# Units of the S5 scan by chunk instead of by quad, and the imaginary sum of each unit on VectorE

## The reference, cut to what matters

```
bu_re = einsum('btgc,gpc->btgp', u, bbar_re);  bu_im likewise
h_t = abar * h_(t-1) + bu_t           (complex, diagonal; associative_scan over t)
y = einsum('btgp,gcp->btgc', h_re, c_re) - einsum('btgp,gcp->btgc', h_im, c_im)
y = gelu(y + d_skip * x);  z = y @ w_glu + b_glu;  out = z[:, :D] * sigmoid(z[:, D:])
```

## Time and profile before

| | |
|---|---|
| median of 3 runs | 1521.61 us (1520.65 to 1522.02) |
| profiled execution | 1522.97 us, its span 1521.1 us |
| TensorE | 1483.9 us busy, 98% of the span |
| VectorE | 1033.6 us, 68% |
| ScalarE | 320.8 us, 21% |
| GpSimd | 90.3 us, 6% |
| chain that ended last | 92% TensorE, 4% VectorE, 2% GpSimd |
| mean granted clock of TensorE | 0.995 of full speed |

### The profile page before, as it was taken

The page is one execution under the profiler, slowest core; times in us unless marked ns, Lnnn a source line. Parts: engine busy times, 40 slices in busy tenths (PEclk is TensorE's granted clock), DMA queues, the critical chain, the costliest instruction groups (busy, mean ns, idle before and its releaser), DMA issues.

```text
span 1521.1 us, 56639 instructions
## 1 busy us (share of the span) xinstructions
PE 1483.9 (98%) x25360; PEld 1098.6 (72%) x25360; DVE 1033.6 (68%) x3653; ACT 320.8 (21%) x598; POOL 90.3 (6%) x71
## 2 busy tenths in 40 slices
PE   9998999999999799999999999999999999999997
PEld 8887889999999687666666666666666666668664
DVE  7787546896875514776766766766667767766665
ACT  2733225677442012001001001001001001001001
POOL 0006202000002700000000000000000000000000
PEclk9999999999999899999999999999999999999999
DMA  8230004444531493979989989989989989999991
GB/s 328 91 131 3 4 4 168 167 167 167 174 132 45 181 390 131 368 273 419 415 327 417 415 332 412 414 340 405 416 345 399 416 351 386 416 362 375 415 368 56
DMA packets 74690, 422.98 MB, mean 278 GB/s; under 512 B 6848, under 2 KB 6976, under 8 KB 39504
## 3 DMA queue, kind: packets, MB, share of 16 engines
q1 hardware_dynamic: 74096, 418.27, 69.5%
q0 software_dynamic: 352, 1.10, 0.2%
HBM read 418.29 MB, written 1.05 MB: 276 GB/s over the span
## 4 chain that ended last, share of the span: by engine, by line
PE 92%; DVE 4%; POOL 2%; issue 1%; ACT 1%; DVEq 0%; POOLq 0%
PE PS L1338 38%; PE PS L1346 19%; PE PS L1147 11%; PE PS L1263 3%; PE PS L776 2%; PE PS L753 2%; PE PS L1370 1%; PE PS L720 1%; PE PS L1132 1%; PE PS L924 1%; PE PS L797 1%; DVE ZI L1608 1%; PE PS L941 1%; PE PS L1253 1%; POOL SPS L2075 1%
## 5 line engine op out<-in xcount | busy, mean ns | idle before, releaser
L1338 PE MATMUL PS<-EXA,XGT 128*32 128x256 f32 x10752 | 611.5, 379 | 0.0
L1965 DVE STREAM_TRANSPOSE MHT<-MHF 32x32 f32<-32x32 f32 x2688 | 544.9, 203 | 40.1
L1338 PEld LDWEIGHTS PS<-EXA,XGT 128*32 128x32 f32 x10752 | 352.6, 110 | 223.1 <-issue 0.4
L1346 PE MATMUL PS<-EXB,MHT 128*32 128x256 f32 x5376 | 321.3, 379 | 1.6 <-DVE MHT L1965 1.6
L1346 PEld LDWEIGHTS PS<-EXB,MHT 128*32 128x32 f32 x5376 | 176.5, 110 | 114.6 <-DVE MHT L1965 2.1
L1960 DVE TENSOR_TENSOR MHF<-MSG,PS 128x128 f32<-128x128 f32 x168 | 48.4, 288 | 239.4 <-ACT MSG L670 238.7
L670 ACT ACTIVATE MSG<-PS 128x128 f32<-128x128 f32 x168 | 46.6, 277 | 764.8 <-PE PS L1338 758.8
L1147 PE MATMUL PS<-FH,WHI 128*128 128x256 f32 x352 | 100.4, 285 | 0.0
L1147 PE MATMUL PS<-FL,WHI 128*128 128x256 f32 x352 | 99.6, 283 | 0.0
L1147 PE MATMUL PS<-FH,WLO 128*128 128x256 f32 x352 | 99.5, 283 | 0.0
L1147 PEld LDWEIGHTS PS<-FH,WHI 128*128 128x128 f32 x352 | 67.5, 192 | 0.2 <-issue 0.2
(11 more groups left out here) (417 smaller groups left out, 1767.8 us busy)
## 6 DMA issues: line engine op xcount, KB each, us to landing
EXA<-in_wmoe SPq DMA_DIRECT2D x112, 2048.0 KB, 18.0
EXB<-in_wmoe SPq DMA_DIRECT2D x224, 512.0 KB, 14.5
FRA<-in_wffn SPq DMA_DIRECT2D x22, 1024.0 KB, 6.0
RING<-in_wsq SPq DMA_DIRECT2D x16, 1024.0 KB, 5.0
FRB<-in_wffn SPq DMA_DIRECT2D x22, 512.0 KB, 3.8
GLUW<-in_wglu SPq DMA_DIRECT2D x8, 1024.0 KB, 12.7
LORA<-in_lora SPq DMA_DIRECT2D x1, 1536.0 KB, 19.3
CON<-in_con SPq DMA_DIRECT2D x1, 1156.0 KB, 21.6
```

The lines of the kernel that those rows point to most:

```text
L1338: mm = pe.matmul(PS[strip(a), GU_BANK[r], 0:T], XGT[:, k, strip(s)], EXA[(2 * quad + e // 2) % RA][:, e % 2, k * T:(k + 1) * T], start=k = ...
L1346: mm = pe.matmul(PS[strip(a), 2 + r // 2, r % 2 * 256:(r % 2 + 1) * 256], MHT[:, i % RB * SLOTS + 32 * s:i % RB * SLOTS + 32 * s + 32], EX ...
L1965: tr = dve.transpose(MHT[strip(q), first:first + 32], MHF[strip(a), strip(q)])
```

## The change

Units 0 to 3 now hold one chunk each (unit c has the four strips of chunk c); units 4 to 7 hold one strip of the four chunks of the second half, as before. The drive is cut up: `drive_chunk(c)` fills 128 columns of four banks (4 to 7 for chunk 1, otherwise 0 to 3), and `drive_quads` makes the second half two chunks at a time. `turn_by` reads units 0 to 3 across four banks, `read_out(0)` waits for one unit for each chunk, and GpSimd and VectorE wait before a slot of PQ only for the chunk that was read from it. VectorE gets the imaginary sum (`imaginary`), after the scans of the next unit; GpSimd makes the two products and the real sum. The tables are laid out in the new order. `first_level` uses banks 2 to 5 and no longer waits for `x_sb`. The core of the diff:

```
             def first_level(g):
-                bank = 2 + 2 * (g % 2)
+                bank = 2 + g
                 pe.wait_ge(S("lt"), g + 1)
-                if g >= 2:
-                    pe.wait_ge(S("x_sb"), g - 1)
...
-            def drive(part):
-                for cc in range(4):
-                    c = 4 * part + cc
-                    if part == 0 or cc == 0:
-                        pe.wait_ge(S("n_out"), 16 + (c + 1 if part == 0 else KC))
...
+            def drive_chunk(c):
+                pe.wait_ge(S("n_out"), 16 + (KC if c == 1 else c + 1))
+                if c >= 2:
+                    pe.wait_ge(S("s_lin"), c if c == 3 else 1)
+                for m in range(2):
+                    for i in range(STEP):
+                        for q in range(NQ):
+                            mm = pe.matmul(PS[:, 4 * (c == 1) + q, m * CHUNKS:(m + 1) * CHUNKS], BBT[STEP - 1 - i][strip(q), m, c, :],
+                                           by_step(HN[strip(q), c, :])[:, :, i], start=i == 0, stop=i == STEP - 1,
+                                           tile_position=(32 * q, 0), skip_group_check=True)
+                mm.then_inc(S("bu_ps"), 1)
+
+            def drive_quads(chunks):
+                pe.wait_ge(S("s_lin"), 2)
+                for c in chunks:
                     for m in range(2):
                         for i in range(STEP):
                             for q in range(NQ):
-                                first = m * T + cc * CHUNKS
-                                mm = pe.matmul(PS[:, 4 * part + q, first:first + CHUNKS], BBT[STEP - 1 - i][strip(q), m, c, :],
+                                first = m * T + (c - 4) * CHUNKS
+                                mm = pe.matmul(PS[:, 4 + q, first:first + CHUNKS], BBT[STEP - 1 - i][strip(q), m, c, :],
...
             def taps(part):
+                pe.wait_ge(S("s_lin"), NQ)
                 for c in range(4 * part, 4 * part + 4):
-                    pe.wait_ge(S("s_lin"), c // 2 + 1)
...
             def read_out(part):
-                pe.wait_ge(S("s_prod"), 16 * (part + 1))
                 for cc in range(4):
                     c = 4 * part + cc
+                    if part == 0:
+                        pe.wait_ge(S("s_prod"), 3 * (c + 1))
+                        pe.wait_ge(S("s_im"), c + 1)
+                    elif cc == 0:
+                        pe.wait_ge(S("s_prod"), 6 * NQ)
+                        pe.wait_ge(S("s_im"), 2 * NQ)
...
-            drive(0)
-            drive(1)
+            drive_chunk(0)
+            drive_chunk(1)
+            drive_chunk(2)
+            drive_quads((4, 5))
+            drive_chunk(3)
+            drive_quads((6, 7))
...
-                bu = PS[:, n, :].rearrange("p (a t) -> p a t", a=2)
                 for x, trig, done in ((SA, COS, "s_ab"), (SB_, SIN, "s_lin")):
-                    tt(x[:, v, :, :], bu, trig[:, n:n + 1, :].to_broadcast([P, 2, T]), ALU.mult).then_inc(S(done), 1)
+                    if n < NQ:
+                        first = 4 if n == 1 else 0
+                        bu = PS[:, first:first + NQ, 0:2 * CHUNKS].rearrange("p q (m t) -> p m q t", m=2)
+                        dest = x[:, v, :, :].rearrange("p m (q t) -> p m q t", q=NQ)
...
+            def imaginary(n):
+                dve.wait_ge(S("s_prod"), 3 * n + 2)
+                if n >= NQ:
+                    dve.wait_ge(S("yq_ps"), n - NQ + 1)
+                tt(PQ[:, n % NQ, 1, :], SPS[:, 0, :], SPC[:, 1, :], ALU.add).then_inc(S("s_im"), 1)
...
                 scan(n)
+                if n > 0:
+                    imaginary(n - 1)
                 if n < 2 * NQ - 1:
                     rotate(n + 1)
+            imaginary(2 * NQ - 1)
...
                 if n > 0:
-                    pool.wait_ge(S("s_prod"), 4 * n)
+                    pool.wait_ge(S("s_prod"), 3 * n)
+                    pool.wait_ge(S("s_im"), n)
                 for x, trig in ((SPC, COS), (SPS, SIN)):
                     tt(x[:, :, :], SGS[:, v, :, :], trig[:, n:n + 1, :].to_broadcast([P, 2, T]), ALU.mult).then_inc(S("s_prod"), 1)
                 if n >= NQ:
-                    pool.wait_ge(S("yq_ps"), 4)
-                pool.wait_ge(S("s_prod"), 4 * n + 2)
+                    pool.wait_ge(S("yq_ps"), n - NQ + 1)
+                pool.wait_ge(S("s_prod"), 3 * n + 2)
                 tt(PQ[:, q, 0, :], SPC[:, 0, :], SPS[:, 1, :], ALU.subtract).then_inc(S("s_prod"), 1)
-                tt(PQ[:, q, 1, :], SPS[:, 0, :], SPC[:, 1, :], ALU.add).then_inc(S("s_prod"), 1)
```

More of the change, by code:

```diff
@@ L1227, in drive @@
                             for q in range(NQ):
-                                first = m * T + cc * CHUNKS
-                                mm = pe.matmul(PS[:, 4 * part + q, first:first + CHUNKS], BBT[STEP - 1 - i][strip(q), m, c, :],
+                                first = m * T + (c - 4) * CHUNKS
+                                mm = pe.matmul(PS[:, 4 + q, first:first + CHUNKS], BBT[STEP - 1 - i][strip(q), m, c, :],
                                                by_step(HN[strip(q), c, :])[:, :, i], start=i == 0, stop=i == STEP - 1,
                                                tile_position=(32 * q, 0), skip_group_check=True)
-                                if cc == 3 and m == 1 and i == STEP - 1:
+                                if c == KC - 1 and m == 1 and i == STEP - 1:
                                     mm.then_inc(S("bu_ps"), 1)
             def taps(part):
+                pe.wait_ge(S("s_lin"), NQ)
                 for c in range(4 * part, 4 * part + 4):
-                    pe.wait_ge(S("s_lin"), c // 2 + 1)
                     for d in range(STEP):
@@ L1252, in read_out @@
                                 out = by_step(PS[strip(q), c // 2, c % 2 * T:(c % 2 + 1) * T])
+                                slot, first = (cc, q * CHUNKS) if part == 0 else (q, cc * CHUNKS)
                                 mm = pe.matmul(out[:, 1:CHUNKS, i], CW[:, i + 1, m, 4 * c + q, :],
-                                               PQ[:, q, m, cc * CHUNKS:(cc + 1) * CHUNKS - 1], start=False,
+                                               PQ[:, slot, m, first:first + CHUNKS - 1], start=False,
                                                stop=i == STEP - 1 and m == 1, skip_group_check=True)
@@ L1602, in _ @@
                 l, g = n0 // 4, n0 % 4
-                bank = 2 + 2 * (n0 % 2)
+                bank = 2 + g if l == 0 else 2 + 2 * (n0 % 2)
                 if l == 0:
@@ L1764, in table @@
                 sin, cos = SIN[:, n, :], COS[:, n, :]
-                tiles = [(slice(cc * CHUNKS, (cc + 1) * CHUNKS), 16 * (n // NQ) + 4 * cc + n % NQ) for cc in range(4)]
+                tiles = [(slice(cc * CHUNKS, (cc + 1) * CHUNKS), 4 * n + cc if n < NQ else 16 + 4 * cc + n - NQ) for cc in range(4)]
                 for own, j in tiles:
@@ L1809, in prepare @@
                     for part in range(2):
-                        own = MAG[:, NQ * part:NQ * part + NQ, :].rearrange("p q (c n) -> p q c n", c=4)
-                        mag = S5T[:, 20, 16 * part:16 * part + 16].rearrange("p (c q) -> p q c", q=NQ)
+                        own = MAG[:, NQ * part:NQ * part + NQ, :].rearrange("p u (b n) -> p u b n", b=4)
+                        mag = S5T[:, 20, 16 * part:16 * part + 16].rearrange("p (c q) -> p c q" if part == 0 else "p (c q) -> p q c", q=NQ)
                         link(dve.tensor_copy(own, mag.unsqueeze(3).to_broadcast([P, NQ, 4, CHUNKS])))
@@ L1846, in turn_by @@
                     dve.wait_ge(S("s_g"), 2 * n - 2)
-                bu = PS[:, n, :].rearrange("p (a t) -> p a t", a=2)
                 for x, trig, done in ((SA, COS, "s_ab"), (SB_, SIN, "s_lin")):
-                    tt(x[:, v, :, :], bu, trig[:, n:n + 1, :].to_broadcast([P, 2, T]), ALU.mult).then_inc(S(done), 1)
+                    if n < NQ:
+                        first = 4 if n == 1 else 0
+                        bu = PS[:, first:first + NQ, 0:2 * CHUNKS].rearrange("p q (m t) -> p m q t", m=2)
+                        dest = x[:, v, :, :].rearrange("p m (q t) -> p m q t", q=NQ)
+                        angle = trig[:, n, :].rearrange("p (q t) -> p q t", q=NQ).unsqueeze(1).to_broadcast([P, 2, NQ, CHUNKS])
+                    else:
+                        bu, dest = PS[:, n, :].rearrange("p (a t) -> p a t", a=2), x[:, v, :, :]
+                        angle = trig[:, n:n + 1, :].to_broadcast([P, 2, T])
+                    tt(dest, bu, angle, ALU.mult).then_inc(S(done), 1)
             def rotate(n):
@@ L1861, in scan @@
                 if n >= 2:
-                    dve.wait_ge(S("s_prod"), 4 * n - 6)
+                    dve.wait_ge(S("s_prod"), 3 * n - 4)
                 for m in range(2):
                     dve.tensor_tensor_scan(SGS[:, v, m, :], MAG[:, n, :], SA[:, v, m, :], 0.0, ALU.mult, ALU.add).then_inc(S("s_g"), 1)
+            def imaginary(n):
[3 more added lines that the diff above has]
```

(1 more changed line is left out.)

## The result

The changed kernel takes 1526.4 us (median of 20 runs, 1518.07 to 1534.27), the kernel before 1519.93 (20 runs, 1517.41 to 1522.68): a ratio of 1.0042 (95% interval 1.0023 to 1.0061), slower where 1512.7 us was forecast. The median hides the shape: ten runs lie between 1518 and 1523 us (median 1521.4), ten between 1530 and 1535 (median 1531.8), and none between. No run took 1526 us. The kernel before has one group. Four executions of the whole series, far off everything else (1564, 1896, 4364 and 5417 us), are disturbed and not used as evidence.

What follows compares the result with a forecast made beforehand. In the mixer both TensorE and the unit chain ended at 527.8, so both must come forward; last read-out from 527.84 to 518.9 gives 8.9 us, 1522.97 to 1514.1, less 1.36 for the median: 1512.7 us, range 1510.8 to 1516.4.

Steps and rivals of the forecast that it cites:

- The start of the units: Mixer: unit 0 needs one drive chunk instead of four, so GpSimd begins at 480.5 instead of 485.71, 5.2 us earlier.
- The time per unit: Mixer's GpSimd and VectorE cycle: 4.86 us per unit instead of 5.09, bounds 3.80 and 5.43; last unit done at 518.2.
- Rival 1: Mixer units: imaginary sum fully on VectorE's cycle, period 5.43, unit 7 ends at 522.2; gain 5.6, 1516.0 us; chance 0.22.
- TensorE's path: Drive, taps, first read-out and GLU half on TensorE without the 8 us hole, ending at 517.0 to 519.2.
- a wait of 0.7 for HN: Drive: after chunk 0 at 475.2 TensorE waits 0.7 us, then 448 records take 13.2 us, ending at 489.0.
- Rival 3: Drive and taps: late units 2 or 3 drop the clock to 0.50, +14 to +23 us, 1526 to 1535; chance 0.03.
- 3.96 us at clock 1.00, to 502.9, or 504.4 with the pause: First read-out: runs at once behind the taps at full clock, 3.96 us; the pause allowed for is 1.48 us.
- the 518.9 that went into the sum: Start of the last read-out, set somewhat later than units at 518.2 and TensorE at 517.0 to 519.2; before, 527.84.
- rival 2: First read-out: TensorE's instructions come slower than they run, two pauses of 1.48 us; gain 7.2, 1514.4 us; chance 0.16.
- The other edits: `first_level` without its VectorE wait: 0, bounds 0 and 0.3 us either way; table, magnitude and slot orders: 0.
- The old hole of 8 us: Kernel before: no matmul from 498.2 to 506.2; read-out behind it at clock 0.50 took 6.33 us, against 3.96 busy.

Runs made afterwards that it cites:

- experiment 2: Changed kernel with three more filler matmuls ahead of chunk 0 of the drive, so chunk 1 follows without a gap; 1522.87 us, ratio 1.0011.
- experiment 11: Changed kernel with filler matmuls, two GLU weight loads at the drive's end, six after the first read-out, imaginary sum back on GpSimd; 1517.52 us.
- experiment 12: Kernel before with one wait moved: chunk 1 of the drive waits for all of HN, a 0.43 us gap; 1532.88 us, ratio 1.0074.
- experiment 5: Changed kernel with filler matmuls and GLU weight loads in two lots, four at the drive's end, four after the first read-out; 1514.95 us, ratio 0.9956.
- 10: Changed kernel with weight loads in two lots of four, without the filler matmuls, so the gap is back; 1527.07 us, ratio 1.0025.
- experiment 4: Changed kernel with the imaginary sum back on GpSimd, gap ahead of chunk 1 still there; 1530.99 us, ratio 1.0057.
- experiment 3: Kernel before with the chunk solve's edit alone (`first_level` on four banks, no wait for VectorE); 1522.45 us, ratio 1.0004.
- experiment 6: Changed kernel with filler matmuls and all eight GLU weight loads only after the first read-out; 1520.15 us, ratio 0.999.
- experiment 7: Changed kernel with filler matmuls and all eight GLU weight loads when the dense FFN is done, beside norm and drive; 1526.6 us, ratio 1.0032.
- 9: Changed kernel with filler matmuls, two GLU weight loads at the drive's end and six after the first read-out; 1517.41 us, ratio 0.997.

## Why the prediction was wrong

**The start of the units: right.** In the changed kernel's trace VectorE's first product came 2.41 us after the drive's start (473.64 - 471.23); forecast 475.78 - 473.29 = 2.49. GpSimd began 478.60 - 471.23 = 7.4 us after it, forecast 7.2, and 6.9 in experiment 2, where the filler makes the drive later and not the units. The products that read four banks take 0.60 us each, as those with one bank: no extra cost.

**The time per unit: right.** Walked 4.86 us, measured 4.93, and 5.12 with the sum on GpSimd. The moved sum saves 0.19 us a unit. The last unit was done at 518.13 against 518.2. Rival 1 (a period of 5.43, with the sum fully on VectorE's cycle) is refuted, and in experiment 11 this part of the change has no worth at the end: the two kernels' medians are 0.1 us apart.

The page of the Trainium skill that doubted such a move (Perfetto Trace Analysis, Optimizing Scalar/DVE Operations) agrees in effect with the runs: 0.19 of 0.72 us is left, and nothing of it in the time.

**TensorE's path: here it failed, in two steps.** The step "a wait of 0.7 for HN" priced that wait at its own length. Rival 3 had the clock fall in the drive and stay low, with 1526 to 1535 us, which takes in the upper group. But it tied the fall to units that come late, and it was given 0.03, because "the gaps that I count are 0.7 us, and the only fall in the mixer stood in a hole of 8 us". So the fall was foreseen, but not its trigger: the clock fell at 476.0, when no unit was late yet. That the time fits is in part luck. Drive and taps lost 36.5 - 24.9 = 11.6 us where the rival has 14 to 23, and the pauses of the read-out, which it left out, made up for the rest. Experiment 12 shows that this one gap of 0.43 us brings the fall in the old order, and experiments 5 and 10, without it and with it, that it does so in the new one. It happens in half of the executions of the changed kernel, in seven of eleven in experiment 4, ten of twelve in 10 and six of six in 12. Two traces have the gap and no fall (4 and 10); what decides between executions was not found.

The second step was "3.96 us at clock 1.00, to 502.9, or 504.4 with the pause". It measured 12.4 us (498.81 to 511.21, experiment 2): 6.67 us of pauses and some 1.5 for the clock lost in them; the GLU half lost another 1.8 (15.77 against 13.97). TensorE's path, 517.0 without a pause in the forecast, became 526.9; against the 518.9 that went into the sum this takes 8.0 of the 8.9 us of gain. This was rival 2, with the right mechanism (the packets in the last section show it) and too small a price: it put two pauses at 1.48 us each, the one of `read_out(1)`, which has next to no DMA beside it. Under the weights' DMA they were 3.92 and 2.75, and the clock on top was not in it. It was given 0.16.

**How the groups come out.** Lower group, with experiment 2 in its place: gain of 8.9 less 8.0, hence about 1521 (forecast 1512.7). Counted from the norm's last matmuls (L737), so that the filler is in, its last read-out starts 55.5 us on, before it was 55.8; 0.3 us of gain is left. The median is nevertheless 1.5 us above the kernel before's, in experiment 2 as in the changed kernel's lower group (1521.4 to 1519.9). Where these 1.5 to 2 us lie was not found. Upper group: the last read-out starts 65.9 us after L737, 10.4 more than in experiment 2, and the groups' medians are 10.4 us apart.

**The other edits: right.** The chunk solve gave nothing (experiment 3).

**The old hole of 8 us** had two sides. It cost the clock of the read-out, which the prediction counted as a gain, and it gave TensorE's instructions time to arrive, which it did not count.

**What the change is worth with the gap filled and the loads in two lots:** 0.9956 (experiment 5), 6.8 us of the forecast 8.9. Its read-out still has 4.3 us of pauses.

## What to carry to other kernels

A wait that is put between small matmuls must be priced by what the granted clock does behind it, not by its length: 0.43 us cost 11, and three filler matmuls removed it. Before a hole on TensorE is closed, look at what else used it. Where idle time is put down to "issue" in a fast stretch of small matmuls, compare its end with the packets of the instruction queue; here the supply of instructions was the bound, and moving four loads behind the read-out was worth 8 us, while the moved sum was worth nothing that could be measured. Where two or more courses of one kernel are possible, look at the single runs, not only at the median.

## What the runs showed of the hardware

**The pauses are TensorE's instructions arriving late.** The profile lists a DMA queue for instructions:

```profile
q8 instruction: 199, 3.26, 0.9%
```

That is 199 packets of 16 KB, one for every 127.4 of the 25360 matmul records on the changed kernel's page, and two pauses in one read-out lie 127 or 128 records apart. The trace has the start and length of each packet. In us from the span's start:

| pause | packet starts | packet ends | TensorE goes on | later by |
|---|---|---|---|---|
| before, last read-out | 529.50 | 530.78 | 532.16 | 1.38 |
| experiment 2, first | 502.27 | 503.27 | 504.68 | 1.41 |
| experiment 2, second | 508.50 | 509.57 | 510.97 | 1.40 |
| experiment 5, first | 501.04 | 502.13 | 503.55 | 1.42 |
| experiment 5, second | 504.83 | 506.05 | 507.52 | 1.47 |
| experiment 6 | 503.56 | 504.49 | 505.78 | 1.29 |
| experiment 12, first | 515.12 | 516.16 | 517.49 | 1.33 |

In the fourteen traces TensorE has 38 pauses of over 0.5 us between 470 and 545 us for which no input was late, among them the 4.57 us of the changed kernel. All 38 end 1.24 to 1.64 us after such a packet; the waits with a cause of their own do not (0.28 to 0.71 us for HN, 2.6 to 13.3 for the units, 3.35 for the first weights).

The weights' DMA makes the packets start later and not last longer. After a pause with the weights at full rate beside it the next packet starts 3.5 to 4.2 us on (eight pauses; 504.68 to 508.50 in experiment 2), without them 1.1 to 1.8 (503.55 to 504.83 in experiment 5). The packets that end the pauses take 0.9 to 1.4 us either way. Even without weights it is 507.52 - 503.55 = 3.97 us from the end of one pause to the end of the next in experiment 5, while the 127 records run in 1.99 us; at the drive's 29.4 ns they take 3.7, close to that time, and the drive has pauses only with the weights beside it (experiment 7). What holds a packet back beside the weights, no record shows.

This is also what the old hole gave. In the kernel before two packets had come ahead of the read-out at 506.27 (ends 496.61 and 502.65), the second of them in the hole. In experiment 2 only the first had (end 497.14) when the read-out began at 498.81.

The sum of the pauses in the first read-out goes with the DMA beside it and just before it: 6.67 us at a DMA share of 1.0 (experiment 2), 4.25 with four loads that are down soon after it begins (5), 2.79 with two that are down before it (9), 1.97 and 1.43 with none beside the taps either (7, 6).

**The clock.** The granted clock fell while TensorE's row said 1.00 busy: at 476.0, in the drive's matmuls of 32 rows by 64 columns, 2.2 us after a gap of 0.43, and in experiment 12 between 479 and 480, again some 2 us after the gap. It did not rise again in the 20 us of drive that were left, and rose in the taps. The Trainium skill (TensorE: Matmul & The Clock Gate, A second HAM failure mode) tells of short idles that come often between groups of matmuls and let the clock swing between its two levels. The traces agree that idles far shorter than a hole can do it, and show a case in which a single one of 0.43 us did.
